# Four blocks of modulation products moved from the front stage into the prompt's attention, and three orders changed in the first sample and the last stage

## What is computed

```python
def _layer_inputs(x, c, w):
    mod = jax.nn.silu(c) @ w['w_ada'] + w['b_ada']          # w_ada: 1024 x 6144
    shift1, scale1, gate1, shift2, scale2, gate2 = jnp.split(mod[:, None, :], N_ADA, axis=-1)
    u = _rmsnorm(x, w['g_attn']) * (1.0 + scale1) + shift1
    qa, ka, va, qb, kc, vc, ks, vs, kw, vw, gn, ga, gb = jnp.split(u @ w['w_in'], SPLIT_AT, axis=-1)
...
def _layer_output(x, o_a, o_cmp, o_sel, o_win, m, ada, w):
    g = m['g_nsa']
    o_b = g[..., 0:1] * o_cmp + g[..., 1:2] * o_sel + g[..., 2:3] * o_win
    y_a = o_a.reshape(B, T, W_A) @ w['w_pa']
    y_b = o_b.reshape(B, T, W_B) @ w['w_pb']
    mixed = (m['g_a'] * y_a + m['g_b'] * y_b) @ w['w_out']
    x = x + gate1 * mixed
    h = _rmsnorm(x, w['g_ffn']) * (1.0 + scale2) + shift2
    a, b = jnp.split(h @ w['w_gu'], 2, axis=-1)
    return x + gate2 * ((jax.nn.silu(a) * b) @ w['w_down'])
```

## Time and profile before

| | |
|---|---|
| median of 3 runs | 1155.56 us (1152.15 to 1156.49) |
| the profiled execution's own time | 1153.42 us |
| its span, first to last instruction | 1151.6 us |
| TensorE matmul busy | 1051.3 us, 91% of the span |
| VectorE / ScalarE / GpSimd busy | 527.6 / 544.1 / 82.7 us |
| mean granted clock of TensorE | 0.95 of full speed |
| moved by DMA | 219.51 MB, 191 GB/s over the span |

### The profile page before, as it was taken

One profiled execution on the slowest core, in us unless ns is written; L12 is line 12 of the kernel. 1 busy time (PEld: TensorE's weight loads), 2 busy tenths in 40 slices (PEclk: granted clock), 3 DMA queues, 4 the chain that ended last, 5 costly groups with the idle time before them and its releaser, 6 DMA issues. The chain is left out here.

```text
span 1151.6 us, 25586 instructions
## 1 busy us (share of the span) xinstructions
PE 1051.3 (91%) x9297; PEld 911.1 (79%) x9297; DVE 527.6 (46%) x1173; ACT 544.1 (47%) x1068; POOL 82.7 (7%) x59
## 2 busy tenths in 40 slices
PE   7789995876999999999999999978998799999997
PEld 3568874656788777878787878777998799999997
DVE  1500015523454546363637363647547755555323
ACT  3422214644566656575656665562543444443223
POOL 1134410000000000000010100000000000000000
PEclk9889996866999999999999999988999899999999
DMA  9787777408557574848384846593654064444501
GB/s 330 216 290 245 253 252 224 174 37 284 186 193 247 174 269 153 283 134 305 128 303 152 290 154 231 158 277 89 195 187 157 24 219 146 146 146 147 183 0 46
DMA packets 129910, 219.51 MB, mean 191 GB/s; under 512 B 19349, under 2 KB 74130, under 8 KB 125059
## 3 DMA queue, kind: packets, MB, share of 16 engines
q1 hardware_dynamic: 124962, 185.14, 48.8%
q0 software_dynamic: 4896, 33.68, 8.0%
HBM read 210.46 MB, written 12.45 MB: 194 GB/s over the span
## 5 line engine op out<-in xcount | busy, mean ns | idle before, releaser
L103 PE MATMUL ps<-b_uH,b_slabH 128*128 128x320 f32 x480 | 150.3, 313 | 9.5 <-DVE b_uL L2340 5.3
L1207 PE MATMUL ps<-t_XT,t_slab 128*128 128x128 f32 x1024 | 145.2, 282 | 10.5 <-DVE t_XT L1654 9.4
L104 PE MATMUL ps<-b_uL,b_slabH 128*128 128x320 f32 x480 | 149.8, 312 | 0.0
L105 PE MATMUL ps<-b_uH,b_slabL 128*128 128x320 f32 x480 | 149.1, 311 | 0.0
L1207 PEld LDWEIGHTS ps<-t_XT,t_slab 128*128 128x128 f32 x1024 | 129.2, 195 | 21.6 <-issue 10.5
L2120 ACT ACTIVATE b_slabH<-t_slab 128x2048 fp32r<-128x2048 f32 (+1 forms) x52 | 92.3, 1783 | 98.3 <-PE ps L105 92.9
L2228 DVE TENSOR_TENSOR b_slabL<-t_slab,b_slabH 128x2048 fp32r<-128x2048 f32 (+1 forms) x52 | 109.1, 2123 | 61.1 <-ACT b_slabH L2120 61.1
L103 PEld LDWEIGHTS ps<-b_uH,b_slabH 128*128 128x128 f32 x480 | 91.6, 191 | 10.1 <-issue 5.7
L1503 ACT ACTIVATE t_KTr<-ps 128x512 f32<-128x512 f32 x152 | 82.2, 592 | 23.2 <-PE ps L1231 20.1
L104 PEld LDWEIGHTS ps<-b_uL,b_slabH 128*128 128x128 f32 x480 | 91.6, 191 | 0.0
L105 PEld LDWEIGHTS ps<-b_uH,b_slabL 128*128 128x128 f32 x480 | 91.4, 190 | 0.0
(11 more groups left out here) (388 smaller groups left out, 2079.9 us busy)
## 6 DMA issues: line engine op xcount, KB each, us to landing
t_Kr<-cache_moba_kv SPq DMA_DIRECT2D x132, 256.0 KB, 3.0
t_Vr<-cache_moba_kv SPq DMA_DIRECT2D x124, 256.0 KB, 5.5
t_slab<-w_ada SPq DMA_DIRECT2D x22, 1024.0 KB, 7.7
t_slab<-w_gu SPq DMA_DIRECT2D x22, 1024.0 KB, 5.2
t_slab<-w_in SPq DMA_DIRECT2D x17, 1024.0 KB, 6.4
t_slab<-w_down SPq DMA_DIRECT2D x11, 1024.0 KB, 5.1
t_slab<-cmp_w SPq DMA_DIRECT2D x2, 2048.0 KB
t_wkv<-cache_nsa_win SPq DMA_DIRECT2D x8, 512.0 KB, 3.2
```

The lines of the kernel that those rows point to most:

```text
L103: pe.matmul(out, w_high, x_high, start=start, stop=False, **kw)
L104: pe.matmul(out, w_high, x_low, start=False, stop=False, **kw)
L105: return pe.matmul(out, w_low, x_high, start=False, stop=stop, **kw)
L1207: return pe.matmul(out[:, P * j:P * j + P], taps(w, j, lp)[:, P * ht:P * ht + P], XT[:, w, lp, j, :, :].rearrange("p v i -> p (v i)"), sta ...
```

## The change

Three parts.

1. `N_LATE` is 4: blocks 8 to 11 (scale2 and gate2) leave the front. Each is now four quarters of 0.5 MB (`load_ada_quarter`: 256 columns and half of the rows), in three buffers (two in `ada_s`, one in `ada_p`), 16 quarters in all. Quarters 0 and 1 are loaded at the end of the front, the others by SyncE in the prompt stage, each when the quarter three before it is used. TensorE runs `ada(0)` between `scores(0)` and `scores(1)`, and `ada(1)`, `ada(2)`, `ada(3)` ahead of `attend(0)`, `attend(2)`, `attend(4)`; each is followed by a `fold` inside that unit. ScalarE has a `vector_copy` and VectorE a `take_fold` for each.
2. The first sequence's first part runs by pairs of quarters: transposes of both, then hidden products of both.
3. In the last stage the first slab is split in three pieces (512, 512, 1024) in place of two; `mix(1, 0)` comes behind the twelve small products; ScalarE takes `high_gu(0, 0)` and `high_gu(1, 0)` inside the run of squares; VectorE's `add_square(m - 1)` comes ahead of `residual(m)`.

```diff
-    N_EARLY, N_LATE = 8, 8
+    N_EARLY, N_LATE = 8, 4
...
+            for n in range(2):
+                load_ada_quarter(sp, t, d, n)
...
+def load_ada_quarter(sp, t, d, n):
+    block, col, half = ADA_FIRST + n // 4, n // 2 % 2, n % 2
+    c0 = 512 * block + 256 * col
+    w_ada = d["w_ada"].rearrange("(k p) n -> p k n", p=P)
+    sp.dma_start(ada_quarter(t, n).rearrange("p (k n) -> p k n", k=4), w_ada[:, 4 * half:4 * half + 4, c0:c0 + 256])\
+      .then_inc(t["ada_landed"][n % 3], 16)
+ADA_FIRST, ADA_BLOCKS = 8, 4
+ADA_BANK = (7, 2, 2, 2)
...
+            def load_ada(n):
+                if n > 2:
+                    sp.wait_ge(ada_used, USED0 + n - 2)
+                load_ada_quarter(sp, t, d, n)
+            load_ada(2)
             sp.wait_ge(t["rows_stored"], 16 * (6 + 2 + NB))
...
+            load_ada(3)
+            load_ada(4)
             for w in range(2):
                 sp.dma_start(w1[:, w, :, :], d["cmp_w1"][w].rearrange("(lp p) n -> p lp n", p=P)).then_inc(w1_landed, 16)
...
+            for n in range(5, 8):
+                load_ada(n)
             sp.dma_start(d["nsa_win_sample"][:, 0:WIN - T, :], d["cache_nsa_win"][:, T:WIN, :]).then_inc(window_kept, 16)
-            sp.wait_ge(window_kept, 16)
+            for n in range(8, 11):
+                load_ada(n)
             for br, outputs in ((BR_MOBA, 2), (BR_SEL, 4), (BR_CMP, CMP_OUT + 2), (BR_WIN, NU + 2)):
                 sp.wait_ge(pv_taken, outputs)
+                if br == BR_CMP:
+                    sp.wait_ge(window_kept, 16)
...
+                for n in {BR_MOBA: range(11, 15), BR_SEL: range(15, 16)}.get(br, ()):
+                    load_ada(n)
...
+            def ada(n):
+                for q in range(4 * n, 4 * n + 4):
+                    col, half = q // 2 % 2, q % 2
+                    pe.wait_ge(t["ada_landed"][q % 3], LANDED0[q % 3] + 16 * (q // 3 + 1))
+                    for g in range(4):
+                        c0 = 32 * (4 * half + g)
+                        last = pe.matmul(ps[ADA_BANK[n]][32 * g:32 * g + 32, 256 * col:256 * col + 256], t["cT"][:, c0:c0 + 32],
+                                         ada_quarter(t, q)[:, 256 * g:256 * g + 256], start=half == 0, stop=half == 1)
+                    last.then_inc(ada_used, 1)
...
                     last.then_inc(pt_tr, 1)
+                meanwhile()
                 done = first_job[u] + jobs_of[u]
...
+            def blocks_within(u):
+                if u == 0:
+                    fold(1)
+                    pe.wait_ge(fold_taken, TAKEN0 + 1)
+                if u == 2:
+                    fold(2)
+                if u == 4:
+                    fold(3)
             scores(0)
+            ada(0)
             scores(1)
             for u in range(NU):
...
                 if u + 2 < NU:
                     scores(u + 2)
-                attend(u)
+                blocks_before(u)
+                attend(u, lambda: blocks_within(u))
...
+                    if job == first_job[u] + 1 and u in (0, 2, 4):
+                        vector_copy(1 + u // 2)
                     pt_copy(job)
...
                 if u + 2 < NU:
                     biased(u + 2)
+                if u in (0, 2, 4):
+                    take_fold(1 + u // 2)
...
-            for q in range(4):
-                segment_transposes(None, 0, q, 0)
-                segment_transposes(None, 0, q, 1)
-                selected_transposes(None, 0, q)
-                hidden_keys(None, 0, q)
-                if q % 2:
-                    selected_scores(None, 0, q // 2)
+            for pair in range(2):
+                for q in (2 * pair, 2 * pair + 1):
+                    segment_transposes(None, 0, q, 0)
+                    segment_transposes(None, 0, q, 1)
+                    selected_transposes(None, 0, q)
+                for q in (2 * pair, 2 * pair + 1):
+                    hidden_keys(None, 0, q)
+                selected_scores(None, 0, pair)
...
             first_gates()
-            mix(1, 0)
             pe.wait_ge(exp_landed, 16)
...
+            mix(1, 0)
             mix(2, 0)
...
-            for i in range(2):
-                high_gu(i, 0)
             act.activation(t["warm"][:, :], t["eps"][:, 0:1], ACT.Sqrt)
             for k in range(KT):
+                if k in (0, 2):
+                    high_gu(k // 2, 0)
                 square(1, k, k)
...
             for m in range(KT):
+                if 2 <= m:
+                    add_square(m - 1)
                 dve.wait_ge(mix_mm, m + 1)
                 residual(m, ps[m % 2], 16, 0, m)
...
-                if 2 <= m:
-                    add_square(m - 1)
```

75 lines of the change are left out of this document (61 added, 14 removed).

## The result

The changed kernel took **1169.26 us** (median of 4 runs: 1160.24, 1168.64, 1169.88, 1170.45) against 1154.81 us before (4 runs, 1152.15 to 1156.49): a ratio of 1.0115, with a 95% interval of 1.0086 to 1.0143. Four more runs of it, with a second profile, gave 1162.18 to 1170.37, median 1165.73, ratio 1.0102 (1.0054 to 1.0150). So it is slower by a little over 1%. The forecast was 1158.5 us, with a range from 1144 to 1168: too low, and the result is just outside its upper end.

The account below looks back on a forecast made before the run. TensorE was taken as busy nearly everywhere, with the prompt stage's small waits deciding. Terms -8.3 + 24.0 - 4.5 - 6.0 - 2.3 = +2.9 us on 1155.56 gave 1158.5 us, own range 1151 to 1166, with rivals 1144 to 1168.

Parts of the forecast that it names:

- What bounds the kernel: Whole kernel: TensorE busy nearly everywhere, so added products cost their time; the prompt stage's chain of small waits decides.
- Front, -8.3: Front: four late blocks save 10.96 us, groups 6 and 8 wait 1.3 us each; 8.3 us less.
- Prompt, the products: Prompt stage: four blocks and folds take 11 to 22 us of TensorE, of which waits could cover half.
- rival (a): Prompt stage: quarters come in time, only products beyond the waits cost, 10 us; 1144.5 us in all, chance 0.2.
- The first wait, 15.5: Ahead of `attend(0)`: quarters 5 to 7 queue behind `cmp_w1`, quarter 7 lands at about 203; 15.5 us more.
- The second wait, 5.2: At unit 2: quarter 11, issued only after unit 1's output is stored, delays the value products by 5.2 us.
- The third, 3.3: At unit 4: quarter 15 needs quarter 12's buffer and lands late, with a fold behind; 3.3 us more.
- First sample, -4.5: First sample: pairs of quarters remove two or three of four TensorE waits, and a gather goes out sooner; 4.5 us less.
- Start of the last stage, -6.0: Last stage: shorter first piece 1.0, wait ahead of `mix(2, 0)` 3.1, small products 1.3, clock 0.6; 6.0 us less.
- Second norm, -2.3: Ahead of the second norm: earlier squares give TensorE 1.3 us, the earlier sum 1.0; 2.3 us less.
- (b): Prompt stage: quarters 11 and 15 land as slowly as in the front, 7.7 us; 1165.5 us in all, chance 0.2.
- (c): From 204 us on: added products keep the clock full, saving 5 us; net -2, 1153.5 us, chance 0.1.

Follow-up runs that it names:

- Without the loads: The changed kernel without the transfers of quarters 3 to 15 and the waits for them (values not right): 1142.2 us, ratio 0.9884 to before.
- The run with the new order: The changed kernel with quarter 5 loaded ahead of `cmp_w1` and quarters 6 and 7 between its halves: 1166.2 us, ratio 1.0113 to before.
- Part 3 alone: The kernel before with only the last stage's edits (three pieces, `mix(1, 0)` moved, two reorderings ahead of the second norm): 1148.3 us, ratio 0.9929.

## Why the prediction was wrong, step by step

Two terms failed. The start of the last stage was to give 6.0 us and gave 0.3 in the profiled execution (0.7 by the first piece, less 0.3 behind it), and code that no edit touches had no term in the sum, though it cost 4.1 us. The prompt stage, the largest term, was right in its mechanism and 2.8 us too small.

- **What bounds the kernel**: right. The chain of small waits in the prompt stage decided most of it, and a product cost its time elsewhere.
- **Front, -8.3**: -7.9, and over all traces with part 1 -7.7 to -10.0. The low part was late there as the step said.
- **Prompt, the products**: too dear. I gave 11 to 22 us of TensorE, of which waits could cover half; rival (a) put the rest at 10. Without the loads 3.2 are left in all.
- **The first wait, 15.5**: the place, the cause and the kind are right: counted from the stage's first product, unit 0's transposes came 18.0 us late and its value products 18.4. It was too small because the quarters landed later than I had them: quarter 3 at 10.7 us and not 9.4, quarter 7 at 29.6 and not 27.4.
- **The second wait, 5.2**: 5.22 for quarter 11, 7.1 with its copy and fold. The step named the store of unit 1 as the gate. The run with the new order shows another one close behind, the copy of the window. I had it and quarters 8 to 10 done "by 220", 9.6 us ahead of TensorE; they landed at 223.0, 224.5 and 225.9, and TensorE came to quarter 8 at 224.74. That no wait shows there is luck.
- **The third, 3.3**: a wait of 1.87, and 1.3 in all. Sum of the three: 18.4 + 7.1 + 1.3 = 26.8 against 24.0.
- **First sample, -4.5**: -4.9; none of the four waits of the earlier trace rows is left, ScalarE's copies end what remains.
- **Start of the last stage, -6.0**: the step that failed. The first piece gave 0.7 of 1.0 (idle 4.23 to 3.57 us). The wait of 3.1 us ahead of `mix(2, 0)` did go. But the small products became longer, not shorter:

```profile
792.14 10.53 PE L2102 MATMUL ps<-t_gn,b_xT 24*128 24x320 f32 x24
```

In the second execution the same row is 8.20 us. The step said that they "stay bound by VectorE", at 0.53 us each. VectorE's multiplications behind them, before and after, say otherwise:

```profile
781.74 5.23 DVE L2254 TENSOR_TENSOR b_oT<-b_oT,ps 128x320 f32<-128x320 f32 x10 [9.76 <-PE ps L1985]
```
```profile
793.09 2.00 DVE L2371 TENSOR_TENSOR b_oT<-b_oT,ps 128x320 f32<-128x320 f32 x4 [2.29 <-PE ps L2102]
795.25 0.49 DVE L2371 TENSOR_TENSOR b_oT<-b_oT,ps 128x320 f32<-128x320 f32 x1 [0.16 <-PE ps L2102]
796.31 0.49 DVE L2371 TENSOR_TENSOR b_oT<-b_oT,ps 128x320 f32<-128x320 f32 x1 [0.58 <-PE ps L2102]
```

Before, ten of twelve follow each other almost without a gap. In the changed kernel four do; from 796.31 on VectorE waits 0.58 us for TensorE ahead of every one, and they come 1.07 us apart, where they came 0.54 apart before. The granted clock is 0.98 from 792 to 795 us and 0.50 from 795 to 802.6: at the low level these products are bound by TensorE. The low level then lasts until 808.4, into `mix(1, 0)`, 13.5 us in all; in the second execution it lasts from 792.6 to 799.4, 6.8 us. "At the full clock" there was also less to win than the 1.3 us I gave, since in the earlier trace rows the 7.71 us ran at a clock of 0.86 already; in none of the sixteen traces are they shorter. So up to the wait for `zL` 3.5 to 4.2 us are won in some executions and none in others: behind the move, "start" was 25.5 to 26.3 us in seven traces and 29.9 to 30.0 in four, with and without the stall, of the changed kernel both. Which of the two an execution gets, no run here explains. Part 3 alone is worth 6.7.
- **Second norm, -2.3**: -2.9, and -1.3 in the second execution.
- **Missing altogether**: the 4.1 us of the loop's row. The sum had a term for each edit and for each place that an edit reaches, and none for code that only moves in memory. What stood there was the stall of 2.67 us and the low clock behind it. The loop's row (5.1) and the start of the last stage (5.3) make up most of the 14.1 us missed in the spans, the prompt stage 2.8.
- **The rivals**: (a) falls, the wait ahead of `attend(0)` was 6.13 us where under 5 would have been its sign. (b) was the nearest in time, 1165.5, for a wrong reason: quarters 11 and 15 landed in 4.9 and 3.5 us, not in 7.7. (c) falls: from 188 to 212 us, in the stage's first wait and behind it, the clock was at the low level, 0.50.
- **The range**: its upper end, 1168, lay 2.5 us above (b)'s middle, with nothing added for an unknown of the kind found here.

## What to carry to other kernels

When a load joins a queue that is full, its own bytes can be the smaller part of its price: what stood ahead of it in the queue, and how few buffers there were to issue it early, cost 20.9 of 26.8 us here, and a fourth buffer with the urgent loads first gave them back. After such a repair look for the next wait in the same queue before you count the gain. And compare the traces also where nothing was edited: instructions added in one stage can cost microseconds in another.

## What the runs showed of the hardware

- TensorE can stand still for its own instructions: 2.42 to 2.97 us at a fixed product of straight code, with the idle time marked "issue", decided by how many instructions stand ahead of it in the program (8 of 8 traces with 133 more have it, 8 of 8 with 0, 197 or 256 more don't). It went on 1.2 to 1.4 us after the end of a 16 KB packet of the queue "instruction".
- A load of 0.5 MB that was issued 0.8 us behind a copy of 4 MB from memory to memory landed after 31.8 us; the same load without the copy ahead of it landed after 7.2.
- Waits on a semaphore that has long been reached aren't free on TensorE: 123 instructions, two waits in each, left it idle for 11.1 us, 0.09 us for one.
- The twelve small products at the same place of the same program took 8.2 us in one execution and 10.5 in another, at a granted clock of 0.82 and 0.68 over the 30 us from the first product of the last stage. One of them takes TensorE 0.53 us at the full clock and 1.07 us at the low level.
